# A two-block trunk on one core: another form of the router's products, its ranks, its mask and the place of the job list

## The reference, cut to what matters

```python
scores = softmax(x @ router_w)                # 512 tokens x 16 experts
sel = scores + router_b
grp_score = sum(top_k(sel.reshape(N, 4, 4), 2)[0], -1)   # best two of each group of 4
gmask = one_hot(top_k(grp_score, 1)[1], 4)               # one group for each token
eidx = top_k(where(repeat(gmask, 4) > 0, sel, -inf), 2)[1]
w = scores[eidx] / sum(scores[eidx])
for e in range(16):
    h = silu(x @ w1[e]) * (x @ w3[e])         # 1024 -> 512
    out = out + gates[:, e:e + 1] * (h @ w2[e])
```

## Time and profile before

| what | value |
|---|---|
| median of 3 runs | 2664.03 us (2663.0 to 2669.01) |
| the profiled execution's own time | 2664.31 us |
| its span, first to last instruction | 2662.5 us |
| mean granted TensorE clock | 0.963 of full |
| TensorE busy | 2521.5 us, 95% of the span |
| VectorE, ScalarE, POOL busy | 944.9, 543.0, 149.8 us |
| matmul passes | 11552 |

### The profile page before, as it was taken

How to read it: one execution, slowest core, us unless ns; L and a number is a source line. 1 busy time by engine, 2 the same in 40 slices (tenths; PEclk the granted TensorE clock), 3 DMA queues, 4 the chain that set the end, 5 groups by cost and what they waited for, 6 DMA issues and landing times.

```text
span 2662.5 us, 31031 instructions
## 1 busy us (share of the span) xinstructions
PE 2521.5 (95%) x11552; PEld 1905.3 (72%) x11552; DVE 944.9 (35%) x1671; ACT 543.0 (20%) x1121; POOL 149.8 (6%) x193
## 2 busy tenths in 40 slices
PE   7999999978999996989899999899999988999999
PEld 3564456567888875867788888665756777888888
DVE  7231266550000003363434542432342343435431
ACT  2300045421111113252211100112212111111100
POOL 1000054201111110000000000000000000000000
PEclk9999999878999998988999999899999999999999
DMA  9301121208989965201223222321220312222321
GB/s 332 103 15 56 38 97 72 80 34 324 330 329 328 332 238 193 62 26 48 64 79 94 81 64 95 111 72 44 75 69 26 95 40 95 80 88 85 89 87 46
DMA packets 83345, 307.12 MB, mean 115 GB/s; under 512 B 9264, under 2 KB 9264, under 8 KB 82624
## 3 DMA queue, kind: packets, MB, share of 16 engines
q1 hardware_dynamic: 75888, 274.24, 30.4%
q0 software_dynamic: 7376, 31.77, 3.0%
HBM read 292.86 MB, written 13.11 MB: 115 GB/s over the span
## 4 chain that ended last, share of the span: by engine, by line
PE 90%; DVE 4%; ACT 3%; issue 2%; DMA 1%; SPq 0%; DVEq 0%; POOL 0%; ACTq 0%; POOLq 0%
PE products L1375 38%; PE products L1222 9%; PE products L867 7%; PE products L1021 7%; PE products L1234 5%; PE products L1280 2%; PE products L1501 2%; PE products L1072 2%; PE products L1445 1%; PE products L931 1%; PE products L1330 1%; PE products L1150 1%; PE products L1040 1%; PE products L975 1%; PE products L882 1%
## 5 line engine op out<-in xcount | busy, mean ns | idle before, releaser
L1375 PE MATMUL products<-normed,ring 128*128 128x264 f32 (+1 forms) x1312 | 303.9, 388 | 11.3 <-DVE normed L2570 11.3
L1375 PEld LDWEIGHTS products<-normed,ring 128*128 128x128 f32 x1312 | 252.1, 193 | 56.1 <-issue 16.0
L1222 PEld LDWEIGHTS products<-arena,ring 128*128 128x128 f32 x2176 | 247.4, 193 | 8.8 <-issue 8.8
L1222 PE MATMUL products<-arena,ring 128*128 128x128 f32 x2176 | 247.7, 276 | 0.8 <-ACT arena L1744 0.8
L1597 ACT ACTIVATE arena<-products 128x512 f32<-128x512 f32 (+4 forms) x253 | 114.3, 471 | 621.7 <-PE products L1021 166.7
L1021 PE MATMUL products<-ring,normed 128*128 128x512 f32 (+1 forms) x416 | 182.5, 599 | 8.4 <-DVE normed L1954 8.4
L1375 PE MATMUL products<-arena,mixed 128*128 128x256 f32 (+1 forms) x832 | 189.4, 382 | 0.0
L1375 PEld LDWEIGHTS products<-arena,mixed 128*128 128x128 f32 x832 | 158.1, 190 | 23.8
L1375 PE MATMUL products<-normed,mixed 128*128 128x264 f32 (+1 forms) x704 | 161.5, 383 | 0.0
L1021 PEld LDWEIGHTS products<-ring,normed 128*128 128x128 f32 (+1 forms) x416 | 73.7, 178 | 115.8 <-issue 115.8
L1375 PE MATMUL products<-arena,normed 128*128 128x264 f32 (+1 forms) x704 | 155.6, 382 | 0.0
(11 more groups left out here) (443 smaller groups left out, 3166.5 us busy)
## 6 DMA issues: line engine op xcount, KB each, us to landing
ring<-in_weights SPq DMA_DIRECT2D x303, 512.0 KB, 4.3
ring<-in_experts SPq DMA_DIRECT2D x204, 512.0 KB, 5.1
arena<-results SPq DMA_DIRECT2D x8, 512.0 KB, 6.5
residual<-in_x POOLq DMA_DIRECT2D x1, 2048.0 KB, 15.8
arena<-in_dft_half POOLq DMA_DIRECT2D x1, 2048.0 KB, 8.4
token_rows<-arena SPq DMA_DIRECT2D x4, 512.0 KB, 2.8
out<-residual SPq DMA_DIRECT2D x8, 256.0 KB, 4.5
arena<-in_bias POOLq DMA_DIRECT2D x1, 1920.0 KB, 24.1
```

The source lines that it names most:

```text
L1222: m = pe.matmul(ps[:, side, m_ * P:(m_ + 1) * P], w[:, k, :], job_t[:, k, :], start=(k == 0), stop=(k == KT - 1))
L1375: m = pe.matmul(bank(p, n), left(k), right(k), start=(fresh and k == 0), stop=(k == kt - 1), skip_group_check=True)
```

## The change

`plan` gains a bank for the logits, between the first and the other seven banks of transposes. Before the norm VectorE makes two constants: `router_w`, the router's weights padded with zeros to 32 columns for each feature tile, and `part_sum`, a 128x16 matrix that adds four groups of 32 partitions. The router's product now holds the 32 columns of feature tile k as the stationary operand, streams the 512 tokens of `h2`, and writes to the 32 partitions that begin at 32 * (k % 4); k and k + 4 accumulate. ScalarE copies the bank to `logit_parts`; four products with `part_sum` add the four groups and turn the result to tokens on partitions. The ranks come from one product of 80 columns and four of 64, 48, 32 and 16. The pair sums take three unlinked additions and one reduction, the mask two instructions. The job list stands behind the one-hot tables, the larger of which is made in two halves, each raising `places`. The gather index is made from the product in four instructions, before the result index.

```diff
@@ -231,7 +231,9 @@
     r["ms_2"], = b.many(1)
     r["mod2"] += b.many(1)
     r["router"], = b.many(1)
-    r["rows"] = b.many(8)
+    r["rows"] = b.many(1)
+    r["logits"], = b.many(1)
+    r["rows"] += b.many(7)
     r["rank"], = b.many(1)
     r["slots"], = b.many(1)
     r["before_jobs"] = b.settle()
@@ -494,6 +496,12 @@
         job_hot = piece(arena, 9216, 2 * ST, JOBS)
         job_of, slot_of = arena[:, 9440:9448], arena[:, 9448:9456]
         result_f, gather_f, slot_t = (arena[:, 9456 + JOBS * i:9456 + JOBS * (i + 1)] for i in range(3))
+        router_w = piece(h_flat, 5632, KT, 32)
+        logit_parts = h_flat[:, 5120:5120 + S]
+        part_sum = tiny[:, 440:440 + EXPERTS]
+        picked = piece(arena, 18200, ST + 1, EXPERTS)
+        pair_sum = piece(arena, 18304, ST * 4, 6)
+        top_two = arena[:, 18400:18400 + ST * 4]
         gather_i = arena[:, 18120:18120 + JOBS].bitcast(U32)
         result_i = arena[:, 18150:18150 + JOBS].bitcast(U32)
         gather_now = arena[:, 18180:18181].bitcast(U32)
@@ -1158,21 +1166,32 @@
                 modulation_2(2, (1, 3))
                 p = r["router"]
                 fill(p)
-                rw = par("router_w").rearrange("p (k e) -> p k e", k=KT)
-                for tt in range(ST):
-                    for k in range(KT):
-                        if tt == 0:
-                            pe.wait_ge(h_ready, 2 * KT + k + 1)
-                        m = pe.matmul(ps[:, p.bank, tt * EXPERTS:(tt + 1) * EXPERTS], h2[:, k, tt * P:(tt + 1) * P], rw[:, k, :],
-                                      start=(k == 0), stop=(k == KT - 1))
+                for k in range(KT):
+
+                    o = 32 * (k % 4)
+                    pe.wait_ge(h_ready, 2 * KT + k + 1)
+                    m = pe.matmul(ps[o:o + 32, p.bank, :], router_w[:, k, :], h2[:, k, 0:S], start=(k < 4), stop=(k >= 4),
+                                  skip_group_check=True)
                 finish(p, m)
 
-                for i, p in enumerate(r["rows"]):
+                def turn_rows(i):
+                    p = r["rows"][i]
                     fill(p)
                     for k in range(4):
                         f, t = 4 * (i % 2) + k, i // 2
                         m = pe.transpose(ps[:, p.bank, k * P:(k + 1) * P], h2[:, f, t * P:(t + 1) * P], ident)
                     finish(p, m)
+
+                turn_rows(0)
+                p = r["logits"]
+                fill(p)
+                read(pe, r["router"])
+                for tt in range(ST):
+                    m = pe.matmul(ps[:, p.bank, tt * EXPERTS:(tt + 1) * EXPERTS], logit_parts[:, tt * P:(tt + 1) * P], part_sum,
+                                  start=True, stop=True)
+                finish(p, m)
+                for i in range(1, 2 * ST):
+                    turn_rows(i)
                 ranks()
 
             def ranks():
@@ -1180,18 +1199,18 @@
                 p = r["rank"]
                 fill(p)
                 pe.wait_ge(chosen, 1)
-                for t in range(ST):
-                    for u in range(t + 1):
-                        pe.matmul(ps[:, p.bank, t * EXPERTS:(t + 1) * EXPERTS], con("earlier") if u == t else ones, rt[11][:, u, :],
-                                  start=(u == 0), stop=(u == t))
+                pe.matmul(ps[:, p.bank, 0:(ST + 1) * EXPERTS], con("earlier"), picked.rearrange("p t e -> p (t e)"), start=True,
+                          stop=False, skip_group_check=True)
                 for u in range(ST):
-                    m = pe.matmul(ps[:, p.bank, 64:64 + EXPERTS], ones, rt[11][:, u, :], start=(u == 0), stop=(u == ST - 1))
+                    to = ps[:, p.bank, (u + 1) * EXPERTS:(ST + 1) * EXPERTS].rearrange("p (t e) -> p t e", e=EXPERTS)
+                    m = pe.matmul(to, ones, bcast(picked[:, u], 1, ST - u), start=False, stop=(u == ST - 1), skip_group_check=True)
                 finish(p, m)
 
                 p = r["slots"]
                 fill(p)
-                pe.wait_ge(places, 1)
                 for i in range(2 * ST):
+                    if i % ST == 0:
+                        pe.wait_ge(places, i // ST + 1)
                     m = pe.matmul(ps[:, p.bank, 0:JOBS], slot_hot[:, i, :], job_hot[:, i, :], start=(i == 0), stop=(i == 2 * ST - 1))
                 finish(p, m)
 
@@ -1728,9 +1747,11 @@
                 for k in range(KT):
                     act.wait_ge(scaled, 2 * KT + k + 1)
                     act.activation(h2[:, k, 0:S], h2[:, k, 0:S], ACT.Identity, bias=mod2[:, 8 + k:9 + k]).then_inc(h_ready, 1)
-                read(act, r["router"])
-                act.activation(rt[1], rt[0], ACT.Exp).then_inc(route_exp, 1)
+                copy(r["router"], logit_parts, bank(r["router"]))
                 for i, p in enumerate(r["rows"]):
+                    if i == 1:
+                        read(act, r["logits"])
+                        act.activation(rt[1], rt[0], ACT.Exp).then_inc(route_exp, 1)
                     copy(p, rows[:, i // 2, (i % 2) * 512:(i % 2 + 1) * 512], bank(p))
 
             def experts():
@@ -2224,9 +2245,15 @@
             def router():
                 modulation_2(1, (2,))
                 link(stt(gain2, mod2[:, 16:24], 1.0, par("norm2_g"), ALU.add, ALU.mult))
+                link(dve.memset(router_w, 0.0))
+                dve.memset(picked[:, ST], 0.0)
+                dve.tensor_copy(router_w[:, :, 0:EXPERTS], par("router_w").rearrange("p (k e) -> p k e", k=KT))
+                link(tt_(part_sum, ident[:, 0:EXPERTS], ident[:, 32:32 + EXPERTS], ALU.add))
+                for o in (64, 96):
+                    link(tt_(part_sum, part_sum, ident[:, o:o + EXPERTS], ALU.add))
                 modulation_2(2, (1, 3))
                 norm(gain2, x[:, :, META:T2], h2, S, rstd[:, 0:S], scaled, "ms_2")
-                p = r["router"]
+                p = r["logits"]
                 ready(dve, p)
                 shifted, e_, score, sel, gs, oh, tmp, selm, o1, o2 = (rt[j] for j in range(10))
                 lg = ps[:, p.bank, 0:64].rearrange("p (t e) -> p t e", t=ST)
@@ -2243,14 +2270,13 @@
                 link(tt_(sel, score, bcast(par("router_b"), 1, ST), ALU.add))
 
                 s4 = sel.rearrange("p t (g e) -> p t g e", g=4)
-                g1, g2 = gs[:, :, 0:4], gs[:, :, 4:8]
-                first = True
-                for a in range(4):
-                    for b in range(a + 1, 4):
-                        link(tt_(g1 if first else g2, s4[:, :, :, a], s4[:, :, :, b], ALU.add))
-                        if not first:
-                            link(tt_(g1, g1, g2, ALU.max))
-                        first = False
+                s16 = sel.rearrange("p t (g e) -> p (t g) e", g=4)
+                for at, step in ((0, 1), (3, 2), (5, 3)):
+                    n = 4 - step
+                    ins = tt_(pair_sum[:, :, at:at + n], s16[:, :, 0:n], s16[:, :, step:4], ALU.add)
+                link(ins)
+                link(dve.tensor_reduce(top_two, pair_sum, AX_X, ALU.max))
+                g1, g2 = top_two.rearrange("p (t g) -> p t g", t=ST), gs[:, :, 4:8]
 
                 link(dve.tensor_reduce(col[3], g1, AX_X, ALU.max))
                 link(tt_(g2, g1, bcast(col[3], 2, 4), ALU.is_equal))
@@ -2258,10 +2284,8 @@
                 link(dve.tensor_reduce(col[4], g2, AX_X, ALU.max))
                 link(tt_(g2, g2, bcast(col[4], 2, 4), ALU.is_equal))
 
-                link(dve.tensor_copy(oh.rearrange("p t (g e) -> p t g e", g=4), bcast(g2, 3, 4)))
-                link(tt_(selm, sel, oh, ALU.mult))
-                link(ts(tmp, oh, 1.0, -NEG, ALU.subtract, ALU.mult))
-                link(tt_(selm, selm, tmp, ALU.add))
+                link(ts(g2, g2, 1.0, -NEG, ALU.subtract, ALU.mult))
+                link(tt_(selm.rearrange("p t (g e) -> p t g e", g=4), s4, bcast(g2, 3, 4), ALU.add))
                 for o, c in ((o1, 5), (o2, 7)):
 
                     link(dve.tensor_reduce(col[c], selm, AX_X, ALU.max))
@@ -2272,8 +2296,8 @@
                     if c == 5:
                         link(stt(selm.rearrange("p t e -> p (t e)"), o.rearrange("p t e -> p (t e)"), 2 * NEG,
                                  selm.rearrange("p t e -> p (t e)"), ALU.mult, ALU.add))
-                oh2, rank = rt[11], rt[12]
-                tt_(oh2, o1, o2, ALU.add).then_inc(chosen, 1)
+                rank = rt[12]
+                tt_(picked[:, 0:ST], o1, o2, ALU.add).then_inc(chosen, 1)
 
                 for o, c in ((o1, 8), (o2, 9)):
                     link(tt_(tmp, o, score, ALU.mult))
@@ -2295,13 +2319,6 @@
                 link(dve.tensor_tensor_scan(end, ones[:, 0:EXPERTS], n_job, 0.0, ALU.mult, ALU.add))
                 link(tt_(first, end, n_job, ALU.subtract))
 
-                over = piece(arena, 17700, JOBS, EXPERTS)
-                link(tt_(over, bcast(end, 1, JOBS), bcast(lane[:, 0:JOBS], 2, EXPERTS), ALU.is_le))
-                link(dve.tensor_reduce(job_e, over, AX_X, ALU.add))
```

(27 more changed lines are left out.)

## The result

| | before | changed |
|---|---|---|
| median, runs side by side | 2666.52 us (4 runs) | 2652.28 us (2650.71 to 2652.66, 4 runs) |
| ratio | | 0.9946, 95% interval 0.9929 to 0.9963 |
| span of the profiled execution | 2662.5 us | 2650.2 us |
| mean granted clock | 0.963 | 0.965 |

The account below looks back on a forecast made before the run. A 44.9 us stretch of latencies from the last shifted tile to the first gathered rows was taken to come off one for one; seven gains and a +2.4 collision sum to -14.1 us, giving 2650.0 us, range 2645.5 to 2656.0.

Parts of the forecast that it names:

- logits: Router product to VectorE's start: passes on four column groups overlap behind the shifted tiles; -7.6 us, bounds -8.5 and 0.
- choice (pair sums and mask): VectorE's steps on the logits: fewer instructions, -1.5 us for the pair sums and -0.5 for the mask.
- ranks: Rank products on TensorE: 28 passes become 10 and their greater width hides; -3.4 us, or -4.6 at full clock.
- rival 2: Loads in the open: each of the router's 16 passes stands load and stream in turn; 2655.9 us, chance 0.04.
- Rivals 1, 2 and 3: Router passes: 1 in line, 2652.7 us (0.15); 2 loads exposed, 2655.9 (0.04); 3 in line at half clock, 2657.8 (0.05).
- preparation: Six new VectorE instructions before the norm: hidden in a 5.99 us wait, cost nothing; without that cover up to 3.6 us.
- row transposes: The other 28 row transposes on TensorE, 4.7 us in all: end by 574, ahead of `chosen`, and cost nothing.
- What then collides: First gather against the first weight tiles: evenly shared DMA makes the gather's 2.4 us 4.8; +2.4, bounds 0 and +3.7.
- Rival 4: Job list too late: weights take the gather's place in full, +3.7 for +2.4; 2651.5 us, inside the forecast's range.
- Rival 5: Slower: logits summed in another order flip a near tie, adding one job's loop turn of 22.30 us; 2672.5, chance 0.02.

Follow-up runs that it names:

- one column group: Changed kernel with all eight router products accumulating on one column group instead of four; 2656.17 us (10 runs).
- old ranks: Changed kernel with the 14 rank products of the kernel before in place of the five; 2659.49 us (10 runs).
- no tile ahead: Changed kernel with no weight tile ahead of the first gather instead of four; 2651.51 us (4 runs).
- list first: Changed kernel with the job list put back ahead of the one-hot tables; 2651.93 us (10 runs).

## Why the prediction was right, and the step that was not

By its own steps, each read between the same two events in both traces:

| step | forecast | before | now | measured |
|---|---|---|---|---|
| last shift to VectorE's start on the logits | -7.6 | 10.93 | 3.09 | -7.8 |
| choice (pair sums and mask) | -2.0 | 9.44 | 7.30 | -2.1 |
| ranks | -3.4 | 5.68 | 2.10 | -3.6 |
| ranks' end to the tables (job list) | -1.8 | 6.56 | 4.84 | -1.7 |
| tables' start to the slots' product | -0.6 | 1.37 | 0.84 | -0.5 |
| slots' product to the gather's issue | -1.1 | 2.96 | 1.81 | -1.2 |
| gather | +2.4 | 4.32 | 7.75 | +3.4 |
| sum | -14.1 | | | -13.5 |

The *logits* lie between the two ends, 2.4 and 4.0 us, as the clock rose with the last product. That neighbouring groups overlap was taken from passes on two groups, and one column group shows it at 2.9 us. The mechanism of rival 2 had a chance of 0.04 and did not occur: the sixteen loads, 0.14 us each, ran under passes of the same rows, and in one column group under passes of the same columns too. The Trainium skill, "TensorE: Matmul & The Clock Gate", section "Part 3: Packing small matmuls — row/col tiling", lets a load overlap only another row group; by that rule, the trace disagrees once more. Rivals 1, 2 and 3 are out by the 3.09 us.

The *preparation* and the *row transposes* cost nothing: VectorE's next wait still was 4.85 us long, and POOL's, SP's and the other readers of `n_jobs` appear in no chain. The *ranks* went by the number of passes and not by their width: 2.10 / 10 = 0.21 us a pass now, 5.68 / 28 = 0.20 before; old ranks gives 3.8 us for the term.

**The step that failed** is *What then collides*, in its size: "Sharing evenly, the gather's 2.4 us become 4.8". The gather's packets do not share from the first byte. The first comes 4.2 us after the issue for 1.6 in an empty machine, 2.6 later, and only then do they take every other turn, which costs the other 0.8. It measured +3.4, near the bound of +3.7. The Trainium skill, "DMA: Bandwidth & Descriptors", section "Queues, rings and completion order", has an engine take turns between the queues it has work for, packet by packet. The trace agrees once the gather has begun (0.23 and 0.20 MB in a microsecond). For the 4.2 us before that, no run shows whether its queue already had work to give.

Rival 4 was put as a mishap inside the range, and it is close to what happened: the move of the list took 1.7 us off VectorE's path and put 3.4 on the gather. With the list back in front the rows land 2.0 us sooner (1.0 sooner by the second turn, as the clock rose later in the first), and in the kernel before the same move is worth 0.2. So one part of the change is a small loss, beside 15.2 us of gain from the others. That the total of -13.5 came so near the -14.1 owes something to luck: the gather cost 1.0 us more than its term, and the other six terms together gained 0.5 more than theirs. The remaining 1.2 us between 13.5 in the stretch and 12.3 in the span is nearly all the later T (1.43), scatter from the attention stage. Rival 5 did not occur: the loop still has 17 turns (x2176 passes).

What stays open is why the gather's first packet waits for tiles of another queue. The reading of the 128 indices or the fetching of its descriptors might stand behind them; no run here separates these.

## What to carry to other kernels

Where a chain of small steps on several engines ends in a long, compute-bound loop, each microsecond off the chain comes off the whole time, and here the durations of before predicted it to 0.2 us a step, wherever no two transfers met. A piece of work moved off such a path must be followed to what it releases: here the list started 2 MB of weights, and these met the one transfer on which everything waited. Ahead of a latency-bound gather ask for no more than has landed by the time its bytes are due; one tile was enough to start the loop.

## What was not expected of the hardware

- A gather of 0.5 MB moved its first packet 1.6 us after its issue with nothing ahead, 4.2 with four weight tiles asked for before it on another queue; from its first packet on, the two queues had about half the engines each.
- Four column groups of float32 products with 512 columns kept up with one tile each 0.67 us at a granted clock of 0.50, where one pass alone takes 0.82 and each product has two.
- The clock of the first turn rose anywhere between 3.0 us (no tile ahead) and 5.8 us (list first) after its start, worth 1.3 us (15.97 to 17.29 for the same 128 passes).
- Weight loads of 0.11 us cost nothing among float32 passes on the same rows and columns: at full clock these followed one another at 0.43 us, as fast as passes of 512 columns did elsewhere (0.425).
